# Splitting the first chunk of an expert's up weights and of its down weights into two transfers of 1 MB

## The reference, cut to what matters

```
for e in range(N_EXPERTS):                            # 32
    hid = xt @ w_up[e] + b_up[e]                      # 1024 x 2048 weights, 8 MB
    x_glu = minimum(hid[:, :1024], 7.0)
    x_lin = clip(hid[:, 1024:], -7.0, 7.0)
    act = x_glu * sigmoid(1.702 * x_glu) * (x_lin + 1)
    y = act @ w_down[e] + b_down[e]                   # 1024 x 1024 weights, 4 MB
    out = out + gates[:, e:e + 1] * y
```

## Time and profile before

| | us |
|---|---|
| median of 3 executions | 1282.92 (1282.23 to 1283.98) |
| profiled execution | 1282.64 |
| its span, first to last instruction | 1280.9 |
| PE busy | 1189.5 (93%) |
| VectorE (DVE) busy | 401.1 (31%) |
| bytes moved | 454.40 MB, of which the experts' weights are 192 transfers of 2 MB |

### The profile page before, as it was taken

The page is one execution under the profiler, slowest core; times in us unless marked ns, Lnnn a source line. Parts: engine busy times, 40 slices in busy tenths (PEclk is TensorE's granted clock), DMA queues, the critical chain, the costliest instruction groups (busy, mean ns, idle before and its releaser), DMA issues.

```text
span 1280.9 us, 15609 instructions
## 1 busy us (share of the span) xinstructions
PE 1189.5 (93%) x5990; PEld 551.5 (43%) x5991; DVE 401.1 (31%) x808; ACT 191.0 (15%) x395; POOL 58.9 (5%) x89
## 2 busy tenths in 40 slices
PE   5899999889999999999999998999999999999995
PEld 1888655354444443333333333333444443333342
DVE  1944364632322222222222222222222232222224
ACT  2200264111111111111111111111111111111111
POOL 2230053000000000000000000000000000000000
PEclk9999999979999999999999999999999999999998
DMA  9973488309499999999999999999699999999690
GB/s 374 373 207 132 158 259 320 126 33 387 179 425 428 428 430 428 427 430 428 427 430 428 427 430 428 427 430 429 250 425 429 428 429 429 428 429 429 264 393 33
DMA packets 49044, 454.40 MB, mean 355 GB/s; under 512 B 16736, under 2 KB 16776, under 8 KB 20320
## 3 DMA queue, kind: packets, MB, share of 16 engines
q1 hardware_dynamic: 48064, 450.90, 85.1%
q0 software_dynamic: 512, 1.72, 0.4%
q10 hardware_dynamic: 448, 1.50, 0.4%
HBM read 453.06 MB, written 1.05 MB: 355 GB/s over the span
## 4 chain that ended last, share of the span: by engine, by line
PE 56%; DMA 39%; DVE 2%; issue 1%; ACT 1%; SPq 0%; POOL 0%; POOLq 0%; DVEq 0%
DMA ring<-in_moe_w_up 37%; PE pair L1207 23%; PE pair L1274 9%; PE pair L1016 8%; PE pair L1133 3%; PE pair L1097 2%; DMA ring<-in_ada_w 2%; PE pair L1032 1%; PE pair L974 1%; PE pair L1042 1%; PE pair L1055 1%; PE pair L1193 1%; PE pair L1215 1%; PE pair L1141 1%; PE pair L1196 1%
## 5 line engine op out<-in xcount | busy, mean ns | idle before, releaser
L1207 PE MATMUL pair<-ring,v_mem 128*64 128x512 f32 x2240 | 502.6, 594 | 41.6 <-DMA ring<-in_moe_w_up 41.2
L1207 PEld LDWEIGHTS pair<-ring,v_mem 128*64 128x64 f32 x2240 | 179.4, 137 | 343.7 <-issue 258.7
L1274 PE MATMUL pair<-ring,v_mem 128*64 128x512 f32 x1120 | 248.0, 594 | 1.4
L908 DVE TENSOR_SCALAR v_mem<-pair 128x512 f32<-128x512 f32 x35 | 24.2, 692 | 408.3 <-PE pair L1215 408.3
L1274 PEld LDWEIGHTS pair<-ring,v_mem 128*64 128x64 f32 x1120 | 92.6, 137 | 132.7 <-issue 132.5
L927 DVE SCALAR_TENSOR_TENSOR hT_low<-pair,v_mem,v_round 128x512 fp32r<-128x512 f32 x35 | 26.3, 751 | 240.4 <-ACT v_round L595 240.4
L581 ACT ACTIVATE v_mem<-v_mem 128x512 f32<-128x512 f32 x35 | 22.0, 629 | 480.5 <-DVE v_mem L908 480.5
L902 DVE TENSOR_TENSOR hT_mem<-hT_mem,pair 128x512 f32<-128x512 f32 x140 | 89.4, 680 | 0.9 <-PE pair L1196 0.9
L1133 PE MATMUL pair<-q_mem,pT_mem 128*64 128x512 f32 x288 | 71.2, 616 | 1.3 <-DVE pT_mem L852 1.3
L595 ACT ACTIVATE v_round<-pair,v_mem 128x512 fp32r<-128x512 f32 x35 | 24.1, 689 | 228.6 <-PE pair L1274 228.6
L381 POOL TENSOR_TENSOR rstd<-ms,neghalf 128x1 f32<-128x1 f32 (+1 forms) x8 | 4.8, 594 | 1066.3 <-DVE ms L631 1066.3
(11 more groups left out here) (225 smaller groups left out, 1054.7 us busy)
## 6 DMA issues: line engine op xcount, KB each, us to landing
ring<-in_moe_w_up SPq DMA_DIRECT2D x128, 2048.0 KB, 23.7
ring<-in_moe_w_down SPq DMA_DIRECT2D x64, 2048.0 KB, 20.8
ring<-in_ada_w SPq DMA_DIRECT2D x24, 1024.0 KB, 9.0
ring<-in_na_w_qkv SPq DMA_DIRECT2D x12, 1024.0 KB, 27.5
ring<-in_na_w_o SPq DMA_DIRECT2D x4, 1024.0 KB, 15.0
tokens<-in_na_rpb SPq DMA_DIRECT2D x32, 96.0 KB, 6.5
gain<-in_norm_g POOLq DMA_DIRECT2D x3, 512.0 KB, 5.8
tokens<-in_x SPq DMA_DIRECT2D x1, 1024.0 KB, 4.9
```

Of the source, the lines that this page charges most:

```text
L908: d.tensor_scalar(glu, bank[0][:, :], LIMIT, None, ALU.min).then_inc(glu_ready, 1)
L1207: last = mm(bank[half][64 * n:64 * n + 64, :], xT[:, k % 4, 64 * (k // 4):64 * (k // 4) + 64], w[:, c0:c0 + HALF], start=k == 0, stop=False)
L1274: last = mm(bank[2][64 * n:64 * n + 64, :], aT[:, j, 64 * half:64 * half + 64], w[:, HALF * n:HALF * n + HALF], start=k == 0, stop=k == KC ...
```

## The change

The two chunks that an expert's block uses first in its up stage and in its down stage (chunk 0 and chunk 4) are loaded as two pieces of 1 MB. A piece is one half of the columns of the chunk, so each of the 128 partitions receives 8 KB, in one ring slot. A list `PIECES` gives chunk, first half and number of halves of each of the now eight transfers of an expert; each has its own arrival semaphore and its own release, so a block releases eight times and the targets of the waits are counted with `PER` = 8. On PE, the first piece of the up weights is released behind the matmuls of k = 0 and the second behind those of k = 1; the first piece of the down weights behind those of k = 1, the second behind those of k = 3. PE waits for the pieces at k = 0 and k = 1 of the up stage and at k = 0 and k = 2 of the down stage. The matmuls and their order are the same.

```diff
-PER, UPS = 6, 4
+UPS = 4
+PIECES = ((0, 0, 1), (0, 1, 1), (1, 0, 2), (2, 0, 2), (3, 0, 2), (4, 0, 1), (4, 1, 1), (5, 0, 2))
+PER, UP_PIECES = len(PIECES), 5
...
-            def load_expert(e, j):
-
+            def load_expert(e, i):
+
+                j, half, halves = PIECES[i]
+                cols = slice(2 * D * half, 2 * D * (half + halves))
                 src = (up_2k[bass.ds(e, 1), j] if j < UPS else down_4k[bass.ds(e, 1), j - UPS])
-                sp.dma_start(expert_chunk(j), src.rearrange("a p n -> (a p) n")).then_inc(expert_in[j], 16)
+                sp.dma_start(expert_chunk(j)[:, cols], src.rearrange("a p n -> (a p) n")[:, cols]).then_inc(expert_in[i], 16)
 
             def expert(e, blocks_before):
-                for j in range(PER):
-
-                    sp.wait_ge(ring_free, blocks_before * PER + (EXP - PER + j + 1))
-                    load_expert(e, j)
-
-            for j in range(PER):
-                sp.wait_ge(ring_free, EXP - RING + 2 * j + 2)
-                load_expert(0, j)
+                for i in range(PER):
+
+                    sp.wait_ge(ring_free, blocks_before * PER + (EXP - PER + i + 1))
+                    load_expert(e, i)
+
+            for i, (j, half, halves) in enumerate(PIECES):
+                sp.wait_ge(ring_free, EXP - RING + 2 * j + half + halves)
+                load_expert(0, i)
...
                 for k in range(KC - 2):
-                    if k % 2 == 0:
-                        expert_chunk_here(pe, e, k // 2)
+                    if k < 2:
+                        expert_piece_here(pe, e, k)
+                    elif k % 2 == 0:
+                        expert_piece_here(pe, e, k // 2 + 1)
                     up(0, k)
                     last = up(1, k)
-                    if k % 2 == 1:
+                    if k == 0 or k % 2 == 1:
                         last.then_inc(ring_free, 1)
...
-                    if j == 0:
-                        expert_chunk_here(pe, e, UPS + half)
+                    if k in (0, 2):
+                        expert_piece_here(pe, e, UP_PIECES + k // 2)
+                    elif k == 4:
+                        expert_piece_here(pe, e, UP_PIECES + 2)
...
-                    if j == 3:
+                    if k in (1, 3, 7):
                         last.then_inc(ring_free, 1)
```

More of the change, by code:

```diff
@@ L212, in chunk_here, with expert_piece_here @@
             eng.wait_ge(slot_in[n % RING], 16 * (n // RING + 1))
-        def expert_chunk_here(eng, e, j):
-            eng.wait_ge(expert_in[j], e * 16 + 16)
+        def expert_piece_here(eng, e, i):
+            eng.wait_ge(expert_in[i], e * 16 + 16)
         def expert_chunk(j):
@@ L1228, in block_step @@
                         make_tables()
-                expert_chunk_here(pe, e, UPS - 1)
+                expert_piece_here(pe, e, UP_PIECES - 1)
                 pe.wait_ge(bsel_ready, b + 1)
```

## The result

The changed kernel takes 1288.07 us (median of 20 executions, 1286.24 to 1291.73) against 1283.19 us for the kernel before (20 executions, 1281.78 to 1288.63). The ratio is 1.0035 with a 95% interval of 1.0028 to 1.0042: 4.9 us slower. The forecast was 1282.3 with a range up to 1286.0.

A forecast was written before the change was run, and what follows sets the result against it. The prediction took the weight stream to bound two runs and PE the rest. A restart gain of -3.4 us and split cost of +2.8 gave -0.6 us, hence 1282.3 us for the median, range 1279.5 to 1286.0.

The forecast's parts named there:

- What bounds the kernel: Whole span: PE's work to the first restart, a transfer run, PE's work, a second run, then PE's work to the end.
- the third restart without effect: At 1216.21, where loads resume after an extra block: experts behind it are bound by PE, so no gain there.
- The earlier release: At restarts after extra blocks, the first load goes out 1.72 us earlier; two of three count, gaining 3.4 us.
- The cost of a split: In the two transfer runs, each chunk loaded as two pieces costs 0.05 us more: 56 splits, 2.8 us (ends 0 and 6.7).
- The 112 us in the prediction: Cost of 56 splits if each paid the Trainium skill's fixed 2.0 us per transfer in full; the prediction rejected it.
- The gain of 1.72 us per restart survives: Behind restarts, new dry times of the queue total 0.5 to 0.6 us against an old 0.5, so the gain stays.
- The sign that was to show it: At the down stage, the first down piece follows the last up chunk with less than 0.6 us of pause.
- the restart gain is lost in bubbles: Rival: behind restarts the queue runs dry up to 1.7 us longer each, only the split cost stays: 1285.7 us; chance 0.06.
- Slow stream: Rival: in the two transfer runs a split costs 0.12 us, lengthening them by 6.7 us: 1286.2 us; chance 0.15.

The follow-up runs named there:

- e3_late: Changed kernel's eight transfers, but PE releases by whole chunks and SP waits once per chunk, as in the kernel before: 1291.01 us, ratio 1.0053.
- e10_two_up_chunks: Changed kernel with chunk 1 of the up weights also in two pieces, each with its own release: 1287.20 us against 1283.27 for the kernel before.
- e2_down_only: Against the kernel before, only the first chunk of the down weights is split, with its early release: 1284.68 us, ratio 1.0008.
- e9_chunk1_later: Kernel before, whole chunks, with chunk 1 released behind k = 4 instead of k = 3, 1.7 us later: 1287.37 us against 1284.20.
- e1_up_only: Against the kernel before, only the first chunk of the up weights is split, with its early release: 1289.38 us against 1283.37.
- e5_row_halves: Kernel before with chunks 0 and 4 each as two transfers of 64 partitions with whole 16 KB rows, released by whole chunks: 1575.92 us against 1284.20.
- e8_down_whole: Kernel before with the down weights in one 4 MB transfer of 32 KB packets, released behind the last down matmul: 1289.44 us against 1283.27.
- e7_all_early: Against the kernel before, all six chunks come in pieces of 1 MB, each released behind its own row group(s): 1295.49 us, ratio 1.0085.

## Why the prediction was wrong, step by step

*What bounds the kernel* was right: two runs paced by the stream, the third restart without effect (tail 85.02 and 84.94), PE's blocks as before, no wait for a first piece in the stream. Its waits are those of the earlier trace rows, the first a little longer:

```profile
505.09 3.65 PE L1211 MATMUL pair<-ring,v_mem 128*64 128x512 f32 x16 [1.08 <-DMA ring<-in_moe_w_up]
509.99 1.94 PE L1211 MATMUL pair<-ring,v_mem 128*64 128x512 f32 x8 [1.24 <-DMA ring<-in_moe_w_up]
```

*The earlier release* was right in its term: 2 x 1.71 us, and without it (e3_late) the loss grows by 3.1 us. The load of the second restart went out at 912.3 and not at 907.3, though: 2.4 us of the difference lie ahead of the first block, 2.6 in the first run.

*The cost of a split* was named rightly and sized too low: 0.077 us where 0.05 was taken, inside the ends given (0 to 0.12). 56 x 0.077 = 4.3 us and not 2.8. By itself this would have left the sum at +0.9 us and the time inside the range. The window of the earlier trace rows counts whole packets over 15 us, and 1% of error in it is 0.05 us a split, as much as the value read from it. The records of the single packets give the cost directly. The 112 us in the prediction rest on a figure for transfers that gpsimd issues; the loads here are issued by SP, and a split cost 0.077 us.

*"The gain of 1.72 us per restart survives"* is the step that failed. The prediction held that a transfer behind an idle or nearly idle queue starts 2.6 us after its issue, and set new bubbles of 0.5 to 0.6 us against an old one of 0.5; so the sum had nothing for them, and nothing for queues that part. The landing times behind the second restart, in the order of the issues at 912.3, 914.0 and 917.5 (compare for a whole chunk):

```profile
DMA to landing us min/median/max: 5.1/5.1/5.1
...
DMA to landing us min/median/max: 6.4/6.4/6.4
...
DMA to landing us min/median/max: 8.7/8.7/8.7
```

The first is in at 917.4, 5.1 us after its issue, as forecast (4.9). The second should have followed 2.5 us later and came 3.0 us later; chunk 1 landed at 926.2, 5.8 us behind it and not 4.9, though it was issued 2.9 us before the second piece was in. The sign that was to show it failed too: the first down piece was in 3.7 us behind the last up chunk (936.10, 939.78), of which 2.5 are its bytes, a pause of 1.2 us where less than 0.6 was forecast. At the down stage (stretch, us, busy times, PE's clock, share of the transfer engines, GB/s) 3 us pass at three quarters of the rate:

```profile
929.00:933.50 4.50, 4.37 (x22) 2.23 (x24) 2.08 (x6) 1.02 (x3) 0.00 (x0) 1.00 1.04 444
934.00:937.00 3.00, 3.00 (x16) 1.21 (x14) 0.00 (x0) 0.00 (x0) 0.00 (x0) 1.00 0.84 317
938.00:941.00 3.00, 3.00 (x18) 1.21 (x16) 1.04 (x3) 0.00 (x0) 0.00 (x0) 1.00 1.07 426
```

My model had one queue that is empty or not. There are 16, and when a transfer is issued close to the end of the one ahead, some of them, here one, can fall behind the others. The lag is not made good before the next gap, and every landing of the run waits for it. The spread grew by 1.4 and 1.2 us over before's 0.69 and 0.97: 2.6 us. Together:

```
                                forecast   measured
release at the restarts            -3.4       -3.4
short packets, 56 splits           +2.8       +4.3   (56 x 0.077)
spread of the 16 queues             0         +2.6
queue dry for all, two restarts     0         +1.1   (the rest)
sum                                -0.6       +4.6   (restart 1 to 3)
```

The last row but one is a remainder, but the landings show it as well. At the second restart the first of the 16 queues landed the first piece and the last down chunk 28.2 us apart (916.62, 944.82) for 11 MB that take 27.1 in the stream, a loss of 1.1 us; before it was 24.7 us for 10 MB of 24.5, a loss of 0.2. At the first restart the loss is 0.9 (342.20 to 370.19), before 0.5. Over both that is some 1.2 us more than before, where the remainder says 1.1. The same sum without free terms gives 7.5 us for e3_late (measured 7.7 from restart 1 to 3), 3.0 for e10_two_up_chunks less its smaller spread, 2.8 (3.3), and for e2_down_only 2.1 of packets, 0.5 less spread and 1.0 less bubble, 0.6 (1.2). For e9_chunk1_later it has 2.9, and 4.6 measured; the 1.5 above are missing from it. e1_up_only has 2.8 us by it and 6.5 measured: there the down weights go out no earlier, so the 3.4 us gained are waited out again at the down chunk, which makes 6.2.

The rival "the restart gain is lost in bubbles" had the place and came near the size (up to 3.4 us lost, where 3.7 were); it got 0.06. Slow stream and lost gain are not alternatives, as the prediction treated them: both happened, and their sum left the range.

What stays open is why a queue falls behind. e9_chunk1_later shows that the moment of one issue is enough. The rest is read from twelve traces (all but e5_row_halves), from the first restart on, by how long before the last landing of the transfer ahead an issue of experts' weights came. Of 60 issues that came 1.9 to 3.9 us before it, 42 were followed by a spread that was larger by 0.2 us or more, up to 2.3; of 55 that came 4.0 to 5.0 us before it, none. So a late issue can part the queues and need not: in the kernel before, the down chunk came 2.3 and 2.5 us before the end and the spread changed by +0.28 and -0.09 us, and e10_two_up_chunks got by with 3.0 us, as said. A queue that was dry for all, as at the down weights of e8_down_whole (issued 0.9 us behind the last landing), did not spread; there it fell to 0.40 us. No run shows the mechanism.

No version beat the kernel before. e10_two_up_chunks shows why: with the spread gone, splits cost 6.5 us and the restarts return 3.4. A split might pay if it were made only for the experts behind an extra block; that was not tried. Nor was another order of an extra block's stages (both blocks' up stages, then both down stages), which would release the up chunks earlier.

## What to carry to other kernels

Where a stream of weights is the bound, a release half a chunk earlier is paid for in every chunk of the stream and earns only where the queue had run dry: count both. Keep the runs per partition long, and count packets rather than transfers. Where a queue starts from empty, issue so that each transfer behind the first has about 4 us of others ahead of it (the bound that the landings of this kernel show): a late one can set back some of the 16 queues, and the whole stretch behind it waits for the last.

## What the runs showed of the hardware that was not expected

- The lag of a queue lasts. In e9_chunk1_later a release 1.7 us later at three restarts made first and last landing 2.2 us apart, still so 250 us later at unchanged rate (429 GB/s).
- A packet of 8, 16 and 32 KB took 0.3136, 0.6148 and 1.2170 us. A straight line through these has about 12 ns beside the bytes. The 4 B packet at the end of a transfer took 9 ns per queue.
- Two transfers of 64 partitions each are no halves of one of 128: 1 MB took 4.9 us each, 319 GB/s over the stream. "SBUF — State Buffer" of the Trainium skill, section "Door 1: The DMA port swizzle", says that partitions 0 to 63 reach only 8 of the 16 ports. As an estimate from this, such a transfer runs at half the rate; the landing times agree (1.05 MB in 4.9 us are 214 GB/s, half of 428).
- TensorE's clock fell behind single waits of 2.9 us, and not behind two shorter ones. In the kernel before PE waits 0.94 and 1.24 us per expert, and the granted clock is 1.00 from 500 to 880 us. With pieces of 1 MB the wait comes in one. In e7_all_early it was 2.83 to 2.91 us eleven times from 500 to 1215 us, and behind eight of these the up matmuls (x8) took 2.55 to 3.63 us where they take 1.94 otherwise; behind three (at 570.49, 898.61 and 1089.36) they took 1.94 all the same. It did not lengthen the run, since PE's next wait was the shorter for it (1.16 to 1.55 us):

```profile
600.32 3.26 PE L1211 MATMUL pair<-ring,v_mem 128*64 128x512 f32 x8 [2.86 <-issue]
...
630.15 1.94 PE L1211 MATMUL pair<-ring,v_mem 128*64 128x512 f32 x8 [1.52 <-issue]
```

  The granted clock over these stretches (last but two of the columns) was 0.79 and 1.00; in the first it stood at the lower of its two levels, 1.2 GHz, for 3.4 us:

```profile
596.00:604.00 8.00, 5.14 (x20) 1.68 (x18) 0.16 (x1) 0.00 (x0) 0.00 (x0) 0.79 1.01 420
604.00:640.00 36.00, 34.13 (x172) 14.77 (x170) 12.33 (x26) 5.67 (x13) 0.00 (x0) 1.00 1.01 422
```
